# A norm's squared feature tiles added up on VectorE, so that TensorE sums one or two tiles instead of eight, in a two-layer hybrid decoder step

## The reference

```
x += 0.5 * SwiGLU_a(rms(x))                                  # ffa13, ffa2
h = rms(x); P = h @ w_in; three branches on P: RWKV, SSD, retention
x += w_out( sum_i sigmoid(P[gate_i]) * (branch_i @ w_branch_i) )   # ret_out, ssd_out, rwkv_out, out
x += CrossAttn(rms(x), memory K/V)                            # K, V of 256 tokens from rms(mem): memk, memv; xq, xo
x += 0.5 * SwiGLU_b(rms(x))                                   # ffb13, ffb2
rms(x) = x * rsqrt(mean(x*x, over the 1024 features) + EPS) * g
```

## Time and profile before

| | us |
|---|---|
| median of 3 runs | 3168.41 |
| lowest, highest | 3164.21, 3170.33 |
| profiled execution: span from its first to its last instruction | 3155.4 |
| median less that span | 13.0 |
| PE busy | 2862.6 (91%) |
| DVE busy | 1815.9 (58%) |
| ACT busy | 1227.8 (39%) |
| POOL busy | 521.6 (17%) |
| mean granted TensorE clock | 0.959 |

### The profile page before, as it was taken

One profiled execution on the slowest core, in us unless ns is written; L12 is line 12 of the kernel. 1 busy time (PEld: TensorE's weight loads), 2 busy tenths in 40 slices (PEclk: granted clock), 3 DMA queues, 4 the chain that ended last, 5 costly groups with the idle time before them and its releaser, 6 DMA issues. The chain is left out here.

```text
span 3155.4 us, 64198 instructions
## 1 busy us (share of the span) xinstructions
PE 2862.6 (91%) x25830; PEld 2656.3 (84%) x25830; DVE 1815.9 (58%) x2810; ACT 1227.8 (39%) x1637; POOL 521.6 (17%) x341
## 2 busy tenths in 40 slices
PE   7998988889989899999989988988899899999997
PEld 7998887777788898799989978877787788988997
DVE  4444767686676565544344347576866765654442
ACT  4534521144332443444254355211543234434542
POOL 0003650054310000000000046401543000000000
PEclk9999999899999999999989999998999989999998
DMA  4444340144373566344344443402354654663442
GB/s 160 147 143 141 113 143 4 33 131 169 96 295 126 181 207 227 121 152 147 114 144 148 145 131 116 127 4 50 115 186 128 245 194 140 220 226 116 152 147 97
DMA packets 119697, 448.22 MB, mean 142 GB/s; under 512 B 13648, under 2 KB 23920, under 8 KB 111664
## 3 DMA queue, kind: packets, MB, share of 16 engines
q1 hardware_dynamic: 97920, 329.75, 33.4%
q0 software_dynamic: 21552, 115.34, 10.0%
HBM read 397.01 MB, written 48.02 MB: 141 GB/s over the span
## 5 line engine op out<-in xcount | busy, mean ns | idle before, releaser
L1546 ACT ACTIVATE w_high<-ring 128x1024 fp32r<-128x1024 f32 x598 | 632.0, 1057 | 789.3 <-PE gemm_banks L889 326.6
L885 PE MATMUL gemm_banks<-in_high,w_high 128*128 128x320 f32 (+1 forms) x2736 | 809.8, 312 | 26.3 <-ACT w_high L1546 13.9
L1942 DVE TENSOR_TENSOR w_low<-ring,w_high 128x1024 fp32r<-128x1024 f32 x436 | 532.3, 1221 | 495.2 <-ACT w_high L1546 494.4
L886 PE MATMUL gemm_banks<-in_low,w_high 128*128 128x320 f32 (+1 forms) x2736 | 799.2, 308 | 0.0
L722 POOL TENSOR_TENSOR w_low<-ring,w_high 128x1024 fp32r<-128x1024 f32 x162 | 414.1, 2565 | 985.6 <-ACT w_high L1546 985.2
L885 PEld LDWEIGHTS gemm_banks<-in_high,w_high 128*128 128x128 f32 x2736 | 517.1, 189 | 34.5 <-issue 14.5
L886 PEld LDWEIGHTS gemm_banks<-in_low,w_high 128*128 128x128 f32 x2736 | 516.9, 189 | 2.7
L889 PE MATMUL gemm_banks<-in_high,w_low 128*128 128x320 f32 (+1 forms) x2736 | 452.6, 308 | 6.1 <-POOL w_low L722 3.9
L889 PEld LDWEIGHTS gemm_banks<-in_high,w_low 128*128 128x128 f32 x2736 | 410.0, 188 | 9.0 <-POOL w_low L722 5.2
L942 PE MATMUL gemm_banks<-in_high,w_high 128*128 128x320 f32 x640 | 207.1, 336 | 22.3 <-DVE arena L2041 16.7
L969 PE MATMUL gemm_banks<-act_high,w_high 128*128 128x320 f32 x704 | 215.2, 319 | 3.3 <-DVE arena L1991 3.3
(11 more groups left out here) (422 smaller groups left out, 4322.9 us busy)
## 6 DMA issues: line engine op xcount, KB each, us to landing
ring<-in_w SPq DMA_DIRECT2D x598, 512.0 KB, 3.6
arena<-in_kc POOLq DMA_DIRECT2D x14, 1024.0 KB, 6.7
arena<-in_vc POOLq DMA_DIRECT2D x14, 1024.0 KB, 6.9
out_fill<-stage SPq DMA_DIRECT2D x80, 160.0 KB, 4.0
arena<-in_ssm POOLq DMA_DIRECT2D x16, 512.0 KB, 13.5
out_s_ssm<-arena POOLq DMA_DIRECT2D x16, 512.0 KB, 14.7
arena<-in_ret POOLq DMA_DIRECT2D x16, 512.0 KB, 22.8
out_s_ret<-arena POOLq DMA_DIRECT2D x16, 512.0 KB, 8.2
```

The source lines that it names most:

```text
L885: mm(dst, w_high[:, slot, w(k)], in_high[:, k, 0:n], start=(k == 0), stop=False)
L886: mm(dst, w_high[:, slot, w(k)], in_low[:, k, 0:n], start=False, stop=False)
L1546: f(w_high[:, slot], ring[:, s, 0:D], ACT.Copy).then_inc(weights_high, 1)
L1942: tt(w_low[:, slot], ring[:, pos % RING, 0:D], w_high[:, slot].bitcast(F32), ALU.subtract).then_inc(weights_split, 1)
```

## The change

The sums over tiles go to DVE, the sum over partitions stays on PE.

- ffa2, ffb2 and xo: DVE adds squared tile 1, then 2, up to 6, to tile 0 as they come (`add_square`). PE sums two tiles behind the last chunk: tile 0 (which holds tiles 0 to 6), and tile 7.
- out: ACT no longer squares x in one piece. It squares tile by tile in the out stage (`squares("out", xsq)`), as in xo, between its weight conversions; DVE adds as in xo, and PE sums two tiles at the old place behind memk.
- mem: DVE halves the squares three times (8 tiles to 4, 2, 1), behind `low_parts("rwkv")`; PE sums one tile.
- start: DVE folds four parts of two tiles into one, and PE sums two tiles.
- xo is no longer a straight run of chunks on PE: it takes the common loop, whose first and fifth chunk have the first chunk's order.

```
-SQUARED = {"ffa2": 0, "xo": KT, "ffb2": 2 * KT}
+SQUARED = {"ffa2": 0, "out": KT, "xo": 2 * KT, "ffb2": 3 * KT}
+ADDED = {"ffa2": "mix", "out": "xattn", "xo": "ffb", "ffb2": "next"}
...
-        n_sq, n_sum = marks("norm_squares", ["mem", "xattn"]), marks("norm_sums", SUMS)
+        n_sq, n_sum = marks("norm_squares", ["mem"]), marks("norm_sums", SUMS)
+        n_add = marks("squares_added", ["mix", "mem", "xattn", "ffb", "next"])
...
-                    if seg in SQUARED and c:
-                        square_sum(seg, c - 1)
-                if seg in SQUARED:
-                    for c in range(count):
-                        chunk(c % RING, c, c == 0)
-                    last_square_sum(seg)
-                    return
                 if seg == "rwkv":
                     for c in range(count):
                         chunk(c % RING, c, "last" if c == count - 1 else c == 0)
                 for c in range(count - count % RING, count):
                     chunk(c % RING, c, False)
-            def square_sum(seg, i):
-                pe.wait_ge(squared, SQUARED[seg] + i + 1)
-                return mm(mp[:, 0, 0:T], K("ones"), nsq[:, i], start=(i == 0), stop=(i == KT - 1))
-            def last_square_sum(seg):
-                ins_ = square_sum(seg, KT - 1)
+            def square_sums(seg, sq):
+                need(n_add, ADDED[seg])
+                mm(mp[:, 0, 0:T], K("ones"), sq[:, 0], start=True, stop=False)
+                pe.wait_ge(squared, SQUARED[seg] + KT)
+                ins_ = mm(mp[:, 0, 0:T], K("ones"), sq[:, KT - 1], start=False, stop=True)
                 if seg == "ffb2":
                     ins_.then_inc(layer_sums, 1)
                 else:
-                    hit(ins_, n_sum, {"ffa2": "mix", "xo": "ffb"}[seg])
+                    hit(ins_, n_sum, ADDED[seg])
...
-                    for i in range(KT - 1):
-                        if (FT * i + FT - 1) // KT == c - 1:
-                            square_sum(seg, i)
-                last_square_sum(seg)
-            def sums(marks_, name, table, src, n=T, waits=(), at_=0):
-                for m, v in waits:
-                    pe.wait_ge(m, v)
-                for k in range(KT):
-                    ins_ = mm(mp[:, at_, 0:n], table, src(k), start=(k == 0), stop=(k == KT - 1))
-                ins_.then_inc(marks_.sem, 1)
-                marks_.hit(name)
-            def norm(tag, sq, n=T):
-                sums(n_sum, tag, K("ones"), lambda k: sq[:, k, :], n, [(n_sq.sem, n_sq.value[tag])],
-                     1 if tag == "mem" else 0)
...
             pe.wait_ge(x_here, 32)
-            for k in range(KT):
-                pe.wait_ge(first_squares, k // 2 + 1)
-                ins_ = mm(mp[:, 0, 0:T], K("ones"), nsq[:, k, :], start=(k == 0), stop=(k == KT - 1))
-            ins_.then_inc(layer_sums, 1)
+            pe.wait_ge(first_added, 3)
+            mm(mp[:, 0, 0:T], K("ones"), nsq[:, 0], start=True, stop=False)
+            mm(mp[:, 0, 0:T], K("ones"), nsq[:, 1], start=False, stop=True).then_inc(layer_sums, 1)
...
-                norm("mem", msq, NMEM)
+                need(n_add, "mem")
+                hit(mm(mp[:, 1, 0:NMEM], K("ones"), msq[:, 0], start=True, stop=True), n_sum, "mem")
                 projection("out", tag="out")
                 projection("memk", NMEM, "mem")
-                norm("xattn", xsq)
+                square_sums("out", xsq)
                 projection("memv", NMEM)
                 projection("xq", tag="xattn")
                 attention()
                 projection("xo", tag="xo")
+                square_sums("xo", nsq)
...
-            def square(seg, i, evacuations):
+            def square(seg, sq, i, evacuations):
                 act_.wait_ge(psum_free, RING + BASE[seg] + evacuations)
-                f(nsq[:, i], x[:, i], ACT.Square).then_inc(squared, 1)
+                f(sq[:, i], x[:, i], ACT.Square).then_inc(squared, 1)
+            def squares(seg, sq):
+                for c in range(KT):
+                    weights(0, RING, SPLIT[RANK[BASE[seg]] + c + AHEAD])
+                    square(seg, sq, c, c + 1)
...
-                stream("out")
+                squares("out", xsq)
                 high_parts("mem", mem, n_full)
-                act_.wait_ge(psum_free, evacuated["out"])
-                A_.mark(f(xsq, x, ACT.Square), n_sq, "xattn")
                 stream("memk")
                 need(n_sum, "xattn")
                 rsqrt(xroot, mp[:, 0, 0:T], xinv, n_root, "xattn")
                 need(at["V"], ("o", len(UNITS) - 1))
                 high_parts("xo", ao)
                 arrived(act_, layer, "stored", SAVES)
-                for c in range(KT):
-                    weights(0, RING, BASE["xo"] + c + AHEAD)
-                    square("xo", c, c + 1)
+                squares("xo", nsq)
...
+                        if 0 < i < KT - 1 and (FT * i + FT - 1) // KT == c - 1:
+                            add_square(seg, nsq, i)
                 dve.wait_ge(psum_free, evacuated[seg])
+            def add_square(seg, sq, i):
+                dve.wait_ge(squared, SQUARED[seg] + i + 1)
+                ins_ = tt(sq[:, 0], sq[:, 0], sq[:, i], ALU.add)
+                if i < KT - 2:
+                    V_(ins_)
+                else:
+                    V_.mark(ins_, n_add, ADDED[seg])
+            def evacuate_squared(seg, sq):
+                b = BASE[seg]
+                for c in range(KT):
+                    dve.wait_ge(chunk_done, b + c + 1)
+                    into_x(1.0)((b + c) % RING, c).then_inc(psum_free, 1)
+                    weights(0, RING, SPLIT[RANK[b] + c + AHEAD])
+                    if c > 1:
+                        add_square(seg, sq, c - 1)
+                dve.wait_ge(psum_free, evacuated[seg])
+            def halve(v, n):
+                half = n // 2
+                return tt(v[:, 0:half], v[:, 0:half], v[:, half:n], ALU.add)
...
             dve.wait_ge(x_here, 32)
+            for part in range(1, 4):
+                dve.wait_ge(first_squares, part + 1)
+                ins_ = tt(nsq[:, 0:2], nsq[:, 0:2], nsq[:, 2 * part:2 * part + 2], ALU.add)
+                ins_.then_inc(first_added, 1)
+                dve.wait_ge(first_added, part)
...
+                    if name == "rwkv_out":
+                        need(n_sq, "mem")
+                        V_(halve(msq, 8))
+                        V_(halve(msq, 4))
+                        V_.mark(halve(msq, 2), n_add, "mem")
...
-                evacuate("out", into_x(1.0))
+                evacuate_squared("out", xsq)
...
-                evacuate("xo", into_x(1.0))
+                evacuate_squared("xo", nsq)
```

More of the change, by code:

```diff
@@ L572, in arrived @@
             eng.sem_inc(waits_taken, 1)
-        squared, first_squares, layer_sums = sem("squared"), sem("first_squares"), sem("layer_sums")
+        squared, first_squares, first_added, layer_sums = sem("squared"), sem("first_squares"), sem("first_added"), sem("layer_sums")
         final_root, final_inv, final_done = (sem(f"final_{n}") for n in ("root", "inv", "done"))
@@ L977, in second_ff @@
                     ins_.then_inc(chunk_done, 3 if c == FT - 1 and seg == "ffa2" else 1)
-                    for i in range(KT - 1):
-                        if (FT * i + FT - 1) // KT == c - 1:
-                            square_sum(seg, i)
-                last_square_sum(seg)
-            def sums(marks_, name, table, src, n=T, waits=(), at_=0):
-                for m, v in waits:
-                    pe.wait_ge(m, v)
-                for k in range(KT):
-                    ins_ = mm(mp[:, at_, 0:n], table, src(k), start=(k == 0), stop=(k == KT - 1))
-                ins_.then_inc(marks_.sem, 1)
-                marks_.hit(name)
-            def norm(tag, sq, n=T):
-                sums(n_sum, tag, K("ones"), lambda k: sq[:, k, :], n, [(n_sq.sem, n_sq.value[tag])],
-                     1 if tag == "mem" else 0)
+                square_sums(seg, nsq)
             def hit(ins_, m, name):
@@ L1602, in silus @@
                                 first_weights("rwkv")
-                            square(second, i, 2 * (i + 1) if i < KT - 1 else FT + (2 if seg == "ffa13" else 0))
+                            square(second, nsq, i, 2 * (i + 1) if i < KT - 1 else FT + (2 if seg == "ffa13" else 0))
             filled = dict.fromkeys(FILLS, 0)
```

## The result

The median of four runs is 3144.85 us (3140.75 to 3147.29), against 3168.53 (3164.21 to 3170.33) for four of the kernel before: a ratio of 0.9925 [0.9910, 0.9940], 23.7 us faster. Timed again beside another set of runs it was 3150.71 (3142.88 to 3154.51, six runs) against 3168.99 (eleven), 0.9936 [0.9918, 0.9953], 18.3 us faster by the medians and 20.3 by the ratio. The forecast was 20.8 us faster and 3147.5; both intervals hold that gain.

A forecast was written before the change was run, and what follows sets the result against it. PE's own order was taken to set the pace in the chunk stages. Terms 14.8 + 4.1 + 5.4 + 0 - 2.4 - 2.1 + 1.0 = 20.8 us took the median from 3168.4 to 3147.6; predicted 3147.5, range 3139 to 3158.

The forecast's parts named there:

- A sum between chunks costs 0.53 us of PE's path, and 28 of them go: ffa2 and ffb2, four stages: seven sums each leave the run of chunks, 14.8 us gained.
- The third rival: Feed-forwards don't profit because weights come by DMA at this pace anyway; 6.0 us gain is left, 3162; chance 0.05.
- xo, 2.05 per layer: xo: six sums save 3.2 us, Ln moves back 1.15 behind the last chunk; 4.1 us gained over two layers.
- xattn, 2.7 per layer: xattn: two sums instead of eight bring Ln 2.7 us earlier; 5.4 us gained over two layers.
- mem, nothing: Memory sums stood in a gap where PE waits for ACT's high inputs at out's start; no gain.
- The clock at out's start, 1.2 per layer: Without the mem sums PE idles and a half-speed stretch follows; 2.4 us lost over two layers, bounds 0 and 3.4.
- out's end, 1.04 per layer: ACT makes memk's high inputs behind out's last square, 1.04 us later, and PE waits; 2.1 us lost over two layers.
- The program's start, 1.0: Start: two sums replace eight, Ln 2.0 us earlier, perhaps a longer slow start of the first chunk; 1.0 us gained.
- What lies around the span (13.0) stays: The 13.0 us around the profiled span stay, so the median goes from 3168.4 to 3147.6.
- the ends eat 9 to 10 us (3157): First rival: half-speed stretches or late DVE additions at stages' ends take 9 to 10 us of the gain; chance 0.14.
- all removed time is gained (34.3 us): Second rival: all sums taken from PE count in full, 34.3 us gained, 3134; chance 0.04.
- The chain of evacuation, square and conversion: Fourth rival: in out and xo each chunk waits for this handover, 5.2 us against 3.52; slower, 3174; chance 0.03.

The follow-up runs named there:

- filler: Changed kernel plus four unread float32 matmuls on PE behind xo's last chunk, ahead of the wait for DVE's addition: 3144.84 us, 0.9924 of the kernel before.
- all three edits: Changed kernel with earlier DVE additions in out and xo, memk's inputs before out's last square, rwkv's second weight chunk converted behind ffa2's norm: 3133.01 us, again 3132.51.
- the third edit: On the changed kernel with early additions and memk's inputs first, ACT converts rwkv's second weight chunk behind ffa2's norm: 0.9891 of the kernel before, again 0.9883.

## Why the prediction held, point by point

**A sum between chunks costs 0.53 us of PE's path, and 28 of them go: right.** Two executions of the changed kernel have ffa2 4.0 to 4.5 us shorter and ffb2 3.2 to 3.8, against 3.7 predicted; doing the sums twice cost 15.5 [11.4, 20]; the feed-forwards alone gave 18.4, interval 12 to 24. What is gained above 3.7 in ffa2 came by the weights: ACT converts rwkv's second chunk, which it got late from its DMA, at 262.73 in place of 268.07, that is 4.2 us earlier when the 1.1 of the start are taken off. Why that DMA came earlier isn't shown; with the feed-forwards alone ffa2 gained 3.8 and 3.7, without a surplus. The third rival (weights by DMA at this pace) is refuted by the 3.52 us per chunk and by the feed-forwards alone.

**xo, 2.05 per layer: mis-sized.** The failed term is "Net 3.2 - 1.15 = 2.05". The order on DVE was right, and so was the sum of tile 0's start. But its two sums were priced at 0.53 each: the wait of 2.19 us ahead of them was in the working, and its effect on the clock was not. Ln stands 4.88 us behind the last chunk's end (1313.68, where the last group of eight started 8 x 0.147 earlier), against 2.50 before: 2.4 later, not 1.15. That leaves 3.2 - 2.4 = 0.8, and the stage is 0.80 shorter in layer 0 of three traces. At full clock, in one layer without a filler and in two with it, Ln stands 3.73 us behind, 1.23 later than before: the 1.15 was right for that case, and the rest is the clock's. A second term was missing: behind this end the first four chunks of ffb13 take 18.44 to 18.79 us in six layers, against 17.42 to 18.29 in ten with the old order, some 0.5 more. With it xo alone has next to nothing left, which is what its times say (at most 0.6 us of gain). The clock is at its lower level for 7.7 to 8.5 us of them, against 5.5 to 6.8 with the old order.

**xattn, 2.7 per layer: right.** Ln has moved to 1.79 us behind the first sum, its table load the last thing ahead of it, and 1.22 us are lost at memv's third chunk. memk, xattn and memv together are 2.7 to 4.2 us shorter in layer 0 and 1.2 to 2.7 in layer 1, the spread being half-speed stretches in memk's first four chunks. Without these four it is 41.08 us before and 38.34 to 38.36 after, in all layers of both executions: 2.7.

**mem, nothing: right.** The rival that the 3.3 us of sums are gained (5.7 for both layers, 0.9982) is excluded by mem alone, 0.9985 to 1.0009.

**The clock at out's start, 1.2 per layer: too dear, and not sure.** It costs 0.9 in the profiled execution and nothing in the one again. These are two executions of one kernel over the same work (first the profiled one, then the one again):

```profile
1123.40:1126.80 3.40, 2.98 (x12) 2.46 (x12) 2.48 (x4) 3.32 (x5) 1.49 (x3) 0.69 0.78 237
```

```profile
1127.20:1130.60 3.40, 2.98 (x18) 2.45 (x18) 2.53 (x4) 3.32 (x5) 1.54 (x3) 1.00 0.87 294
```

PE, DVE and ACT are busy alike, and the clock is 0.69 in one and 1.00 in the other. A wait makes a half-speed stretch possible, and it doesn't make it certain: such a term should be priced between nothing and its full cost. In the eight traces with this start of out the 0.9 stands in 6 of 16 layers.

**out's end, 1.04 per layer: right.** It is 0.95 to 1.03 in five profiles with the change's order, and 0.0 in four with memk's inputs first. Left out was that behind the longer wait memk more often starts slow (7 layers of 10 against 4 of 18), 1.4 us each time.

**The program's start, 1.0: right.** The first matmul of the first chunk starts 1.7 us earlier, and of that 1.1 are left at the fifth (1.7 in the execution again).

**"What lies around the span (13.0) stays": wrong.** Every run that lists a span has 1.5 to 1.7 us around it. With as much around it, the profiled execution of before (span 3155.4) took about 3157 us: an unusually fast one, below all of the 55 timed runs of before. No cost stood around it. It did no harm, because the sum was a difference, taken off the median as well as off the span. But by the spans alone the gain would have come out as 13.2 us, which is what two single executions of a kernel with a spread of 20 us can tell.

**That the sum came out so near** (20.8 against 23.7 and 18.3) is luck in part: over both layers xo's gain was put up to 2.5 us too high and some 1 us in ffb13's first chunks was left out, while out's start was put 0.7 to 2.4 us too dear and ffa2 gained about 1 us more than its sums.

**The rivals.** That the ends eat 9 to 10 us (3157) is refuted as a whole, and in its kind it is true: xo's end (1.2 per layer by the clock) and out's start are such losses, some 2.4 to 4.2 us in all. That all removed time is gained (34.3 us) lies outside both intervals. The chain of evacuation, square and conversion never paces out: with that part alone out's first four chunks take 14.95 us against 15.03. A wait for low weights at out's third chunk, a sign that the prediction had named, does stand in the execution again, 0.31 us, but it stood there before as well, 0.39 us.

## What to carry to other kernels

Price the removal of work by where it stands: between back-to-back chunks every piece counts in full, in a gap it counts nothing, and at a stage's end only the order behind the last chunk counts. If a wait remains there, price the few matmuls behind it at half speed too, as the upper bound; an addition or a conversion moved ahead of the last handover then can pay twice. And where one execution differs from the next by 10 us, compare stage by stage between the traces before a gain is put down to an edit.

## What had not been expected of the hardware

**DVE held up by POOL.** In the kernel with all three edits one scalar_tensor_tensor of the norm, usually about 0.5 us, took 2709 ns. The group in the stretch 264.5 to 266.8 (busy us, mean ns):

```profile
L1942 DVE SCALAR_TENSOR_TENSOR arena<-arena,par 128x320 f32<-128x320 f32 x1 | 2.7, 2709 | 0.0
```

POOL's subtraction of low weights ran from 264.24 for 2.35 us, so DVE's instruction (from 264.23) ended 0.35 us behind POOL's. It is no single case: in the kernel before, at 385.14, a scalar_tensor_tensor of the same shape (L2088) took 2.59 us beside a POOL subtraction, and the next one 0.55. But at this norm the two hadn't met before the third edit. The Trainium skill, SBUF — State Buffer, section on SBUF's two separate sides, says that a DVE instruction with two SBUF inputs and a POOL instruction that reads SBUF exclude each other for a whole instruction; this row agrees, at 2.2 us of delay.

**How much one kernel varies.** The two profiled executions of the changed kernel differ by 7.8 us in span (3142.2, 3150.0) at the same mean clock, 0.954, with one and the same program. The stretch from rwkv to rwkv_out, which no edit touches beyond its first chunk, takes 818 to 831 us in fourteen traces. What decides whether a stretch runs at half speed these runs don't show.
